# Moving the mLSTM value transposes between other tiles of TensorE, and splitting the last head's x in two spans

## The chip, the cores and the metric

The kernel runs on one core of a Trainium2 chip. The metric is the device time of one execution in microseconds. Before the change the median of three runs is 2675.86 us (2675.53 to 2677.09).

## The reference, cut to what matters

The model is two blocks in a row on 512 tokens of width 1024. The first is an RWKV-7 layer and a forgetting-attention layer with their MLPs. The second is an mLSTM layer followed by a Fourier layer. The change touches only the first stage of the mLSTM layer, which computes, for each of 4 heads of width 512 and for 768 tokens (256 context and 512 latent ones):

```
xm     = h @ w_in                       # per head: 512 channels x 768 tokens
xconv  = silu(conv3x3(xm) + b)          # depthwise; context tokens as one row
q, k   = xconv @ w_q, xconv @ w_k       # scores = (q k^T), latent queries x all keys
v      = xm                             # values, needed with tokens on the partitions
gates  = q @ wq_g + k @ wk_g + v @ wv_g # input and forget gates
```

The chunked scan with gates, the output norm and the projection follow in a later stage. The kernel keeps channels on the partitions, folds w_q and w_k into one 512 x 512 matrix per head (so that scores are xconv^T (W xconv)), and must transpose xm to get the values.

## The kernel before, in words

All large products are computed in three passes of a split precision: each operand is a high part (fp32r) and a low part (what the high part leaves), and hi*hi, hi*lo and lo*hi are summed in PSUM. So each activation needs two instructions, one that writes the high part (ScalarE) and one that subtracts it (VectorE or GpSimd), and GpSimd does the same for the weights: `whi` (L500), then `wlo` (L502), a ring of two blocks.

**The stage.** It is one block of the program, from about 1641 us to 1933 us of the profiled execution. Each engine has its own list, written out in program order, and the engines meet at semaphores only. For head h = 0..3, TensorE does:

1. "xm" of head h+1: 8 tiles (4 groups m of 128 channels, each with a 256-token and a 512-token tile), 24 matmuls per tile (L554), from two weight blocks. Head 0's own tiles were made before the loop.
2. "v" of head h: 6 tiles of 4 fp32 transposes each (L2774), a tile being 128 tokens x 512 channels.
3. "q" of head h: 4 tiles of 12 matmuls (L2784), from `xch` and `xcl`, the high and low parts of the convolved x.
4. The gate sums of head h, 24 groups in PSUM banks 4 and 5 (L2798).
5. "s", the scores of head h: 6 tiles (one per 128 keys) of 12 matmuls (L2806), from `xch`, `xcl` as weights and `qk_h`, `qk_l`.

All tiles but the gate sums go through a ring of four PSUM banks (NACC = 4), in the order of the list `order`. A tile may begin when the tile four places ahead of it in that list has been taken: `acc_taken` counts reads by ScalarE, and `low_made` counts the low parts of q by VectorE.

**ScalarE** reads xm tiles out (L2815, `xm_tile`), then the value tiles: it needs a row sum first, so that vsb = 512 * v - sum(v). For head 0 it makes the sum itself (L2875, with an accumulated output) and then the read (L2878). For heads 1 and 2 VectorE makes the sum (`value_sum`, L2981). For head 3, VectorE does both for tiles 0 and 1, and the sums of the others. Then ScalarE sends `vsb` to DRAM, makes the high parts of q (L2833), reads the scores (L2815 again) and between the last four of them does `silu` of the next head (L2823) with its DMA; after all six it makes `xch` of the next head (`high_x`, L2828, four instructions over all 768 tokens).

**VectorE** makes the low parts `xcl` (L2992, heads 1 and 2), then the convolution of the next head, four groups m of eleven instructions on PSUM banks 6 and 7 (L2958, L2957) and a copy (L2972). Inside the group m = 2 of the heads 1 and 2 the six `value_sum` stand between the taps, and inside m = 3 the four `low_of` of q (L3002). After them come the gate sums (L3031). For head 3, where no convolution is left, it waits for the last score of head 2 (`taken("s", h - 1, 5)`), then does value tiles 0 and 1, `xcl` of groups 2 and 3, and the other sums. GpSimd makes `xcl` of head 0, and of head 3's groups 0 and 1 (L2719).

So head 3's x, of which TensorE reads the same `xch`/`xcl` buffers as head 2, can be split only when the last score of head 2 is done, and q of head 3 waits for that.

Of the kernel before, what the change touches and what calls it, by code (L numbers as in the profile page):

```python
# [377 lines left out]
def program(nc, A, out, plan, vat, cat):  # L378
    ctx = ExitStack()
    with ctx:  # L380
# [2281 lines left out]
        read_place = {what: j for j, what in enumerate(w for w in order if w not in low_place)}  # L2662
        phase_start()
        with nc.Block() as block:
# [17 lines left out]
            head_gates_in = signal("head_gates_in")  # L2682

# [32 lines left out]
            def _(pool):  # L2716
# [12 lines left out]
                low(3, 0)  # L2729
                low(3, 1)  # L2730
# [3 lines left out]
            def _(pe):  # L2734
# [13 lines left out]

                def xm_of(h):
                    for j in range(2):  # L2750
                        if h == 0 and j == 0:
                            block_by_tile(pe, firsts["xm0"][1], h2h, h2l, h_ready, tokens=spans, bank_free=bank_free)
                            continue
                        block_of(pe, firsts[f"xm{h}"][1] + j, 0, h2h, h2l, KT, 256, tokens=spans, bank_free=bank_free)
# [12 lines left out]
                for h in range(HM):  # L2767
# [1003 lines left out]
```

## Time and profile before

| | us |
|---|---|
| median of 3 runs | 2675.86 |
| the profiled execution's own time | 2674.32 |
| its span (first to last instruction) | 2672.5 |
| TensorE (PE) busy | 2551.9 (95%) |
| VectorE (DVE) busy | 1309.9 (49%) |
| ScalarE (ACT) busy | 734.8 (27%) |
| GpSimd (POOL) busy | 1462.3 (55%) |
| mean granted TensorE clock | 0.973 of full |

Rows of the timeline give the start, the duration, the engine and line, what is written from what, and in brackets how long the engine had been idle and which instruction released it. Matmuls overlap their successors, so the time that one costs is the distance between two starts (0.227 us for 512 columns in this stage) and not its duration (0.39 us).

### The profile page before, as it was taken

The numbers are of one execution on the slowest core, as the hardware profiler recorded it, in microseconds if no ns is written. First come the engines' busy times: TensorE is split into PE (matmuls) and PEld (weight loads), VectorE is DVE, ScalarE is ACT, GpSimd is POOL, SyncE is SP. The second block draws the span as 40 slices with busy tenths as digits, with TensorE's granted clock in tenths as the row PEclk, the third lists the DMA queues.
The fourth block names the chain that finished last, engine by engine and source line by source line (L and its number), as shares of the span: only waits on it lengthen the run. The fifth ranks groups of instructions, "written<-read, shape, count | busy, mean of one in ns | idle before, by whom it ended". The sixth has DMA issues, their size and how long they took to land. (4 is left out here: it accounts for less than half of the span.)

```text
span 2672.5 us, 36710 instructions
## 1 busy us (share of the span) xinstructions
PE 2551.9 (95%) x15042; PEld 2037.0 (76%) x15042; DVE 1309.9 (49%) x1880; ACT 734.8 (27%) x1381; POOL 1462.3 (55%) x472
## 2 busy tenths in 40 slices
PE   5899989999999999999999999999899999999998
PEld 4677778788888886657888887788676578877787
DVE  7737337675662241453845526977285634131212
ACT  4644332231120221452311212323323422011210
POOL 3663633477777665206777763433272037754674
PEclk9999989999999999999999998999999999999999
DMA  6221433656653221103555522222243345222121
GB/s 270 96 73 60 121 92 155 271 216 230 230 220 110 87 103 65 69 1 130 210 214 218 214 99 97 103 111 111 103 166 113 129 166 229 95 79 77 64 101 72
DMA packets 89903, 358.80 MB, mean 134 GB/s; under 512 B 27288, under 2 KB 41112, under 8 KB 52384
## 3 DMA queue, kind: packets, MB, share of 16 engines
q1 hardware_dynamic: 64992, 227.65, 23.8%
q10 hardware_dynamic: 24768, 129.12, 12.9%
q8 instruction: 106, 1.74, 0.3%
q14 instruction: 37, 0.30, 0.0%
HBM read 317.66 MB, written 39.06 MB: 133 GB/s over the span
## 5 line engine op out<-in xcount | busy, mean ns | idle before, releaser
L500 POOL TENSOR_TENSOR whi<-wraw,con_sb 128x2048 fp32r<-128x2048 f32 x166 | 600.2, 3616 | 1072.2 <-PE ps L554 755.9
L502 POOL TENSOR_TENSOR wlo<-wraw,whi 128x2048 fp32r<-128x2048 f32 x166 | 783.0, 4717 | 13.0
L554 PE MATMUL ps<-hh,whi 128*128 128x512 f32 x952 | 373.0, 392 | 6.0 <-POOL wlo L502 6.0
L554 PE MATMUL ps<-hh,wlo 128*128 128x512 f32 x952 | 371.4, 390 | 0.0
L554 PE MATMUL ps<-hl,whi 128*128 128x512 f32 x952 | 371.4, 390 | 0.0
L554 PEld LDWEIGHTS ps<-hh,whi 128*128 128x128 f32 x952 | 179.4, 188 | 47.4 <-POOL wlo L502 6.4
L2165 DVE TENSOR_TENSOR midl<-rsq,midh 128x512 fp32r<-128x512 f32 x64 | 155.9, 2441 | 112.6 <-ACT midh L2122 112.6
L554 PEld LDWEIGHTS ps<-hh,wlo 128*128 128x128 f32 x952 | 179.3, 188 | 37.5
L554 PEld LDWEIGHTS ps<-hl,whi 128*128 128x128 f32 x952 | 179.5, 189 | 37.0
L554 PE MATMUL ps<-midh,whi 128*128 128x512 f32 x512 | 200.0, 391 | 0.0
L554 PE MATMUL ps<-midh,wlo 128*128 128x512 f32 x512 | 199.7, 390 | 0.0
L554 PE MATMUL ps<-midl,whi 128*128 128x512 f32 x512 | 199.6, 390 | 0.0
L554 PE MATMUL ps<-h2h,whi 128*128 128x512 f32 (+1 forms) x480 | 177.9, 371 | 0.7 <-ACT hb L3307 0.7
L554 PE MATMUL ps<-h2l,whi 128*128 128x512 f32 (+1 forms) x480 | 176.6, 368 | 0.0
L554 PE MATMUL ps<-h2h,wlo 128*128 128x512 f32 (+1 forms) x480 | 176.5, 368 | 0.0
L2025 DVE SCALAR_TENSOR_TENSOR cond_w<-cond_w,ps 128x1024 f32<-128x1024 f32 x136 | 159.8, 1210 | 0.0
L2116 ACT ACTIVATE relu<-ps 128x512 f32<-128x512 f32 x64 | 38.2, 598 | 381.2 <-PE ps L554 347.9
L2171 DVE SCALAR_TENSOR_TENSOR x<-ps,mod,x 128x512 f32<-128x512 f32 x64 | 48.0, 750 | 190.5 <-PE ps L554 190.5
L554 PEld LDWEIGHTS ps<-midl,whi 128*128 128x128 f32 x512 | 96.5, 189 | 20.1
L554 PEld LDWEIGHTS ps<-midh,wlo 128*128 128x128 f32 x512 | 96.4, 188 | 20.1
L554 PEld LDWEIGHTS ps<-midh,whi 128*128 128x128 f32 x512 | 96.5, 189 | 19.9
L2957 DVE SCALAR_TENSOR_TENSOR ps<-xm,vec_sb,ps 128x441 f32<-128x441 f32 (+3 forms) x160 | 105.0, 656 | 4.8
(477 smaller groups left out, 4804.8 us busy)
## 6 DMA issues: line engine op xcount, KB each, us to landing
wraw<-wst SPq DMA_DIRECT2D x162, 1024.0 KB, 4.8
cond_w<-wcond ACTq DMA_DIRECT2D x68, 1024.0 KB, 4.8
first_w<-wcond SPq DMA_DIRECT2D x8, 1024.0 KB, 19.6
mod_w<-wcond SPq DMA_DIRECT2D x8, 1024.0 KB, 13.9
d_v<-key_and_query ACTq DMA_DIRECT2D x4, 1536.0 KB, 5.7
d_s<-ssb ACTq DMA_DIRECT2D x4, 1536.0 KB, 5.3
sld<-d_s SPq DMA_DIRECT2D x4, 1536.0 KB, 8.3
vld<-d_v SPq DMA_DIRECT2D x16, 384.0 KB, 3.5
```

Of the source, the lines that this page charges most:

```text
L500: pool.tensor_tensor(whi[:, s], wraw[:, f], C("zero").broadcast_to([P, BLK]), ALU.add).then_inc(sem("w_high"), 1)
L502: pool.tensor_tensor(wlo[:, s], wraw[:, f], whi[:, s].bitcast(F32), ALU.subtract).then_inc(w_split, 1)
L554: o = e.matmul(ps[:, b, :nt], w[:, k, mc], x[:, k0 + k, t0:t0 + nt], start=first and k == 0 and j == 0, stop=final and k == nk - 1 and j == 2)
L2025: o = dve.scalar_tensor_tensor(cond_w[n % 2][:, m], cond_w[n % 2][:, m], 1.0, row_at[r], ALU.mult, ALU.mult, accum_out=cond_to[layer][2 * ...
L2116: act.activation(relu[:, n % 4], ps[:, b], ACT.Relu).then_inc(*AC.up(acc_free[b]))
L2165: dve.tensor_tensor(midl[n // KT % 2][:, n % KT], rsq[:, n % 4], midh[n // KT % 2][:, n % KT].bitcast(F32), ALU.subtract).then_inc(*mid_lo ...
L2171: dve.scalar_tensor_tensor(x_sb[:, m], ps[:, b], mod[layer][:, 40 + m:41 + m], x_sb[:, m], ALU.mult, ALU.add).then_inc(*VE.up(acc_free[b]))
L2957: dve.scalar_tensor_tensor(dst, src, w(kh, kw), dst, ALU.mult, ALU.add).then_inc(*VE.up(chain))
```

## The change

- The values of heads 0, 1 and 2 are transposed two tiles at a time behind the groups m = 1, 2, 3 of the next head's xm tiles. ScalarE makes sum and read of them all, in the same order; VectorE's `value_sum` leaves the convolution.
- The values of head 3 are transposed one tile at a time behind each of head 2's score tiles. VectorE sums and reads them (`last_value_taken`).
- The scores of head 2 are done in the order 2, 3, 4, 5 (latent keys), 0, 1 (context keys). The `silu` of head 3 stand behind the first four. The high part of its x is made in two spans: the 512 latent tokens after the fourth score has been read, the 256 context tokens after the sixth. VectorE makes the low parts in the same two spans (`last_lows`), with value tiles 4 and 5 between them. GpSimd makes none of head 3.
- q of head 3 waits for the latent low parts, k by k; the gate sums wait for the context low parts. xm blocks are issued in four quarters instead of two halves.

```diff
         order = [("xm", 0, n) for n in range(8)]
+        V_BEHIND = {1: (0, 1), 2: (2, 3), 3: (4, 5)}
+        def score_order(h):
+            return (2, 3, 4, 5, 0, 1) if h == HM - 2 else range(6)
         for h in range(HM):
-            order += [("xm", h + 1, n) for n in range(8) if h + 1 < HM]
-            order += [(what, h, n) for what, many in (("v", 6), ("q", 4), ("s", 6)) for n in range(many)]
+            for m in range(4):
+                if h + 1 < HM:
+                    order += [("xm", h + 1, 2 * m), ("xm", h + 1, 2 * m + 1)]
+                    order += [("v", h, n) for n in V_BEHIND.get(m, ())]
+            order += [("q", h, n) for n in range(4)]
+            for i, n in enumerate(score_order(h)):
+                order += [("s", h, n)] + [("v", HM - 1, i)] * (h == HM - 2)
...
+                if (what, h) == ("v", HM - 1):
+                    return last_value_taken.at(n + 1)
...
-                low(3, 0)
-                low(3, 1)
                 split_weights(pool, ahead(*names)[1])
...
+                    for m in range(4):
+                        block_of(pe, firsts[f"xm{h}"][1] + m // 2, 0, h2h, h2l, KT, 256, tokens=spans, m0=m % 2, mn=1,
+                                 tell=m % 2 == 0, bank_free=bank_free)
+                        for n in V_BEHIND.get(m, ()):
+                            turn_values(h - 1, n)
...
-                    for s in range(6):
-                        b = tile_bank()
-                        for m in range(4):
-                            o = pe.transpose(ps[:, b, P * m:P * m + P], xm[:, m, P * s:P * s + P], ident)
-                        o.then_inc(*PE.up(acc_ready))
-                    pe.wait_ge(*PE.need(sem("xc_ready"), 4))
+                    if h < HM - 1:
+                        pe.wait_ge(*PE.need(sem("xc_ready"), 4))
...
+                            if h == HM - 1 and m == 0:
+                                pe.wait_ge(*last_low[0].at(k + 1))
...
+                    if h == HM - 1:
+                        pe.wait_ge(*last_low[1].at(4))
...
-                    for s in range(6):
+                    for i, s in enumerate(score_order(h)):
...
+                        if h == HM - 2:
+                            turn_values(HM - 1, i)
...
+                def value_read(h, n):
+                    b = bank()
+                    act.wait_ge(*AC.need(acc_ready))
+                    act.activation(vsb[:, n], ps[:, b], ACT.Copy, scale=-1.0,
+                                   accum_out=vsum[:, n:n + 1]).then_inc(*v_summed.inc())
+                    act.wait_ge(*v_summed.at(6 * h + n + 1))
+                    act.activation(vsb[:, n], ps[:, b], ACT.Identity, bias=vsum[:, n:n + 1],
+                                   scale=512.0).then_inc(*AC.up(acc_taken))
...
+                        if h == HM - 2:
+                            AC.skip(acc_ready, 1)
+                            turn["evac"] += 1
+                            if i < 4:
+                                silu(h + 1, i)
+                            if i == 3:
+                                for m in range(4):
+                                    high_x(m, LAT)
...
-                        if h:
-                            conv(h + 1, 2, lambda s: value_sum(h, s))
-                        else:
-                            conv(1, 2)
+                        conv(h + 1, 2)
                         conv(h + 1, 3, lambda n: low_of("q", h, n))
                     else:
-                        dve.wait_ge(*taken("s", h - 1, 5))
-                        for s in range(2):
-                            value_sum(h, s)
-                            value_read(h, s)
-                        low(h, 2)
-                        low(h, 3)
-                        for s in range(2, 6):
-                            value_sum(h, s)
+                        for n in range(4):
+                            value_sum(h, n)
+                            value_read(h, n)
+                        last_lows(0, LAT)
+                        for n in range(4, 6):
+                            value_sum(h, n)
+                            value_read(h, n)
+                        last_lows(1, CX)
```

TensorE in the scores of head 2, before: the end of the last score tile (`qk_h`, `qk_l`, `xch`, `xcl`), the values of head 3 (24 transposes of `xm_12908`) and the first matmuls of its q (L2784).

```order
L2806 MATMUL ps<-qk_h,xch 128x512
L2806 MATMUL ps<-qk_l,xch 128x512
L2806 MATMUL ps<-qk_h,xcl 128x512
L2774 MATMUL ps<-con_sb,xm_12908 128x128 x24
L2784 MATMUL ps<-xch,whi 128x512
L2784 MATMUL ps<-xcl,whi 128x512
L2784 MATMUL ps<-xch,wlo 128x512
```

After the change, the same engine in the scores of head 2 (L2830 is the score line now, L2766 the transpose line):

```order
L2830 MATMUL ps<-qk_h,xch 128x512
L2830 MATMUL ps<-qk_l,xch 128x512
L2830 MATMUL ps<-qk_h,xcl 128x512
L2766 MATMUL ps<-con_sb,xm_12908 128x128 x4
L2830 MATMUL ps<-qk_h,xch 128x512
L2830 MATMUL ps<-qk_l,xch 128x512
L2830 MATMUL ps<-qk_h,xcl 128x512
L2830 MATMUL ps<-qk_h,xch 128x512
L2830 MATMUL ps<-qk_l,xch 128x512
L2830 MATMUL ps<-qk_h,xcl 128x512
```

The 24 transposes of head 3 stand in six groups of four behind the six score tiles, and q begins behind the last group. In the same way each of the three groups of 24 transposes of heads 0 to 2 is now three groups of eight between xm tiles.

VectorE at the end of the stage, before: the two sums and reads of value tiles 0 and 1 (`key_and_query` is the buffer of the values), two low parts of x, four sums, and the first low part of q:

```order
L2981 TENSOR_REDUCE vsum<-ps 128x1
L2987 TENSOR_SCALAR key_and_query<-ps,vsum 128x512
L2981 TENSOR_REDUCE vsum<-ps 128x1
L2987 TENSOR_SCALAR key_and_query<-ps,vsum 128x512
L2992 TENSOR_TENSOR xcl<-xc_third,xch 128x768
L2992 TENSOR_TENSOR xcl<-xc_fourth,xch 128x768
L2981 TENSOR_REDUCE vsum<-ps 128x1 x4
L3002 TENSOR_TENSOR qk_l<-ps,qk_h 128x512 x4
```

And after the change, from the sum of value tile 3 on:

```order
L3016 TENSOR_REDUCE vsum<-ps 128x1
L3022 TENSOR_SCALAR key_and_query<-ps,vsum 128x512
L3029 TENSOR_TENSOR xcl<-xc,xch 128x512 x2
L3029 TENSOR_TENSOR xcl<-xc_third,xch 128x512
L3029 TENSOR_TENSOR xcl<-xc_fourth,xch 128x512
L3016 TENSOR_REDUCE vsum<-ps 128x1
L3022 TENSOR_SCALAR key_and_query<-ps,vsum 128x512
L3016 TENSOR_REDUCE vsum<-ps 128x1
L3022 TENSOR_SCALAR key_and_query<-ps,vsum 128x512
L3029 TENSOR_TENSOR xcl<-xc,xch 128x256 x2
L3029 TENSOR_TENSOR xcl<-xc_third,xch 128x256
L3029 TENSOR_TENSOR xcl<-xc_fourth,xch 128x256
```

All six sums and reads are VectorE's now, and the eight low parts are those of 512 latent tokens, then those of 256 context tokens, with value tiles 4 and 5 between them.

## Rows read from the trace of the kernel before

**Rows 1.** Part 1 of the page: busy time of each engine, share of the span.

```profile
PE 2551.9 (95%) x15042; PEld 2037.0 (76%) x15042; DVE 1309.9 (49%) x1880; ACT 734.8 (27%) x1381; POOL 1462.3 (55%) x472
```

**Rows 2.** Waits of TensorE, 1700 to 1933 us: total, times, longest.

```profile
PE ps L2784 <- ACT key_and_query L2878: 7.3, 4, 5.7
...
PE ps L2806 <- DVE qk_l L3002: 0.3, 1, 0.3
```

**Rows 3.** Timeline of TensorE: first value transposes and first q matmul, heads 0, 1, 3.

```profile
1710.68 1.91 PE L2774 MATMUL ps<-con_sb,xm 128*128 128x128 f32 x16
...
1715.52 0.47 PE L2784 MATMUL ps<-xch,whi 128*128 128x512 f32 x1 [0.73 <-ACT key_and_query L2878]
...
1780.84 1.91 PE L2774 MATMUL ps<-con_sb,xm 128*128 128x128 f32 x16
...
1785.46 0.47 PE L2784 MATMUL ps<-xch,whi 128*128 128x512 f32 x1 [0.32 <-ACT key_and_query L2878]
...
1886.61 1.91 PE L2774 MATMUL ps<-con_sb,xm 128*128 128x128 f32 x16
...
1896.69 0.77 PE L2784 MATMUL ps<-xch,whi 128*128 128x512 f32 x1 [5.67 <-ACT key_and_query L2878]
```

**Rows 4.** Timeline of ScalarE: the value sums of two tiles of head 0.

```profile
1711.38 0.59 ACT L2875 ACTIVATE key_and_query<-ps 128x512 f32<-128x512 f32 x1
...
1712.68 0.59 ACT L2875 ACTIVATE key_and_query<-ps 128x512 f32<-128x512 f32 x1
```

**Rows 5.** Timeline of TensorE: gate sums and first scores, heads 0, 1, 2, 3.

```profile
1726.61 0.64 PE L2798 MATMUL ps<-xm,value_gate 128*32 128x256 f32 x8
...
1731.01 0.50 PE L2806 MATMUL ps<-qk_h,xch 128*128 128x512 f32 x1 [0.32 <-DVE qk_l L3002]
...
1800.55 0.50 PE L2806 MATMUL ps<-qk_h,xch 128*128 128x512 f32 x1
...
1869.57 0.61 PE L2798 MATMUL ps<-xcl,folded_w 128*32 128x512 f32 x4
1870.11 0.50 PE L2806 MATMUL ps<-qk_h,xch 128*128 128x512 f32 x1
1870.45 0.40 PE L2806 MATMUL ps<-qk_l,xch 128*128 128x512 f32 x1
...
1910.65 0.64 PE L2798 MATMUL ps<-xm,value_gate 128*32 128x256 f32 x8
```

**Rows 6.** Timeline of VectorE: the last low part of q, heads 0 and 1.

```profile
1730.27 0.68 DVE L3002 TENSOR_TENSOR qk_l<-ps,qk_h 128x512 fp32r<-128x512 f32 x1
...
1797.28 0.69 DVE L3002 TENSOR_TENSOR qk_l<-ps,qk_h 128x512 fp32r<-128x512 f32 x1 [0.21 <-ACT qk_h L2833]
```

**Rows 7.** Windows, busy time by engine, clock: head 0 of the convolution, head 1's transposes.

```profile
1661.00:1735.00 74.00, 72.06 (x423) 59.95 (x423) 70.14 (x101) 24.84 (x45) 40.12 (x12) 1.00 0.32 118
...
1781.00:1786.00 5.00, 3.60 (x27) 2.83 (x25) 4.52 (x8) 2.78 (x5) 0.00 (x0) 1.00 0.01 2
```

**Rows 8.** Timeline of VectorE, 1750 us: three low parts of x in head 1.

```profile
1750.86 6.78 DVE L2992 TENSOR_TENSOR xcl<-xc,xch 128x768 fp32r<-128x768 f32 x2 [15.18 <-ACT xch L2828]
1757.56 0.95 DVE L2992 TENSOR_TENSOR xcl<-xc_third,xch 128x768 fp32r<-128x768 f32 x1
```

**Rows 9.** Timeline of GpSimd, same time: high and low part of a weight block.

```profile
1747.92 3.60 POOL L500 TENSOR_TENSOR whi<-wraw,con_sb 128x2048 fp32r<-128x2048 f32 x1 [23.45 <-PE ps L554]
1751.60 5.22 POOL L502 TENSOR_TENSOR wlo<-wraw,whi 128x2048 fp32r<-128x2048 f32 x1
```

**Rows 10.** Timeline of TensorE: two other idle times, at 2040 and 1992 us.

```profile
1992.18 0.80 PE L3211 MATMUL ps<-con_sb,gnat 4*128 4x4 f32 x6 [3.31 <-DVE nm L3474]
...
2040.69 1.10 PE L3193 MATMUL ps<-pp,vld 128*128 128x512 f32 x2 [2.39 <-DVE pp L3438]
```

**Rows 11.** Windows, granted clock right behind those idle times (third number from the end).

```profile
1992.00:1996.00 4.00, 3.82 (x24) 2.63 (x24) 0.36 (x2) 0.00 (x0) 0.00 (x0) 0.50 0.24 92
...
2040.70:2042.00 1.30, 1.08 (x2) 0.25 (x2) 1.23 (x3) 0.00 (x0) 0.00 (x0) 1.00 0.34 114
```

More of the change, by code:

```diff
@@ L2661, in program @@
         low_place = {what: j for j, what in enumerate(parted_tiles)}
-        read_place = {what: j for j, what in enumerate(w for w in order if w not in low_place)}
+        read_place = {what: j for j, what in enumerate(
+            w for w in order if w not in low_place and w[:2] != ("v", HM - 1))}
         phase_start()
@@ L2682, in program @@
             head_gates_in = signal("head_gates_in")
+            last_value_taken = signal("last_value_taken")
+            last_low = [signal(f"last_low_made{j}") for j in range(2)]
             h_items = [("ctx", k) for k in range(KT)] + [("lat", k) for k in range(KT)]
@@ L2747, in tile_bank, with turn_values @@
                     return b
-                def xm_of(h):
[L2750 to L2754, printed above, removed]
+                def turn_values(h, n):
+                    b = tile_bank()
+                    for m in range(4):
+                        o = pe.transpose(ps[:, b, P * m:P * m + P], xms[h % 2][:, m, P * n:P * n + P], ident)
+                    o.then_inc(*PE.up(acc_ready))
+                def xm_of(h):
+                    if h == 0:
+                        block_by_tile(pe, firsts["xm0"][1], h2h, h2l, h_ready, tokens=spans, bank_free=bank_free)
+                        block_of(pe, firsts["xm0"][1] + 1, 0, h2h, h2l, KT, 256, tokens=spans, bank_free=bank_free)
+                        return
+                    for m in range(4):
[3 more added lines that the diff above has]
+                            turn_values(h - 1, n)
                 fold_product(pe, 14, 0)
@@ L2864, in _ @@
                             high_x(m + 2)
-                    if h:
-                        act.wait_ge(*AC.need(sem("v_sent"), 16))
-                    for s in range(6):
-                        b = bank()
-                        act.wait_ge(*AC.need(acc_ready))
-                        if h == HM - 1 and s < 2:
-                            continue
-                        if h == HM - 1 and s == 2:
-                            act.wait_ge(*taken("v", h, 1))
-                        if h == 0:
-                            act.activation(vsb[:, s], ps[:, b], ACT.Copy, scale=-1.0,
-                                           accum_out=vsum[:, s:s + 1]).then_inc(*v_summed.inc())
-                        act.wait_ge(*v_summed.at(6 * h + s + 1))
-                        act.activation(vsb[:, s], ps[:, b], ACT.Identity, bias=vsum[:, s:s + 1],
-                                       scale=512.0).then_inc(*AC.up(acc_taken))
+                        if h + 1 < HM and m in V_BEHIND:
+                            if h and m == 1:
+                                act.wait_ge(*AC.need(sem("v_sent"), 16))
+                            for n in V_BEHIND[m]:
+                                value_read(h, n)
                     act.wait_ge(*taken("v", h, 5))
@@ L2885, in _ @@
                         act.wait_ge(*AC.need(sem("s_sent"), 16))
-                    for s in range(6):
+                    for i, s in enumerate(score_order(h)):
                         read_out(ssb[:, s], T, scale=KS)
-                        if h + 1 < HM and s >= 2:
+                        if h == HM - 2:
[4 more added lines that the diff above has]
+                            if i == 3:
+                                for m in range(4):
+                                    high_x(m, LAT)
+                        elif h + 1 < HM and s >= 2:
                             silu(h + 1, s - 2)
-                    act.wait_ge(*taken("s", h, 5))
+                    if h == HM - 2:
+                        for m in range(4):
+                            high_x(m, CX)
+                    act.wait_ge(*taken("s", h, score_order(h)[5]))
                     act.dma_start(d_s[h], ssb[:]).then_inc(*AC.up16(sem("s_sent")))
-                    if h + 1 < HM:
+                    if h + 2 < HM:
                         for m in range(4):
@@ L2974, in value_sum @@
                 def value_sum(h, s):
-                    if s >= 6:
-                        return
                     n = place["v", h, s]
@@ L2987, in value_read, with last_lows @@
                     dve.tensor_scalar(vsb[:, s], ps[:, place["v", h, s] % NACC], 512.0, vsum[:, s:s + 1], ALU.mult,
-                                      ALU.add).then_inc(*VE.up(acc_taken))
+                                      ALU.add).then_inc(*last_value_taken.inc())
+                def last_lows(j, part):
+                    for m in range(4):
+                        dve.wait_ge(*xc_high(HM - 1 + j, m))
+                        dve.tensor_tensor(xcl[:, m, part], xcs[m][:, part], xch[:, m, part].bitcast(F32),
+                                          ALU.subtract).then_inc(*last_low[j].inc())
                 def low(h, m):
```

6 lines of the change are left out of this document (3 added, 3 removed).

## The prediction

> **What bounds the kernel now.** I read the page's busy times first: TensorE (PE) is busy 2551.9 us, 95% of the span, and no other engine reaches 56% [rows 1]. So a change is worth what it takes from TensorE's idle time and from its time at the low clock, unless another engine then decides. Second I read TensorE's own waits inside the stage that the change touches: of all its idle time, the largest item is at the first matmul of q (L2784), 7.3 us in four waits, the longest 5.7, all for ScalarE's reads of the value tiles. At the scores only 0.3 us is waited, for VectorE's low part of q [rows 2]. Third, the timeline around these places gives what each costs.
>
> From the first transpose of a head to the first matmul of its q it takes 1715.52 - 1710.68 = 4.84 us in head 0, 4.62 us in head 1, and 1896.69 - 1886.61 = 10.08 us in head 3 [rows 3]. Head 2 repeats head 1 to the hundredth, so there are two of 4.62. The transposes themselves need little of it: sixteen take 1.91 us when nothing holds them [rows 3], so 24 take at most 2.87; since 1.91 contains the last one's tail once, I estimate 2.62 us. The rest is the ring of four banks: a value tile is made in some 0.44 us (a sixth of 2.62), but read by ScalarE only every 1.30 us, from 1711.38 to 1712.68 [rows 4].
>
> **The change part by part.**
>
> *Heads 1 and 2, values behind the xm tiles.* The same 24 transposes are issued per head, so 2.62 us stay. What goes is the wait: 4.62 - 2.62 = 2.0 us a head. What is late next? ScalarE now makes sum and read of two tiles, 2 x 1.30 = 2.6 us, in each of three groups of TensorE work that last 24 x 0.12 + 24 x 0.227 = 8.3 us plus eight transposes of 0.9; with the two xm reads of about 1 us it is less than half busy. The ring asks that a tile four places back was read: behind value tiles it is the xm pair of the same group, and for the next pair it is the xm pair of the group before. Before q the four tiles are xm 6, xm 7, v 4 and v 5, and q's third tile, the first that needs v 4, begins 5.4 us after q starts. So no bank holds TensorE, and I cost the ring at nothing; if that cover were gone the price is 1.3 us a tile.
>
> The other thing that can be late is VectorE. In head 1 its last low part of q ended at 1797.28 + 0.69 = 1797.97, and the scores began at 1800.55 [rows 5, 6]: 2.6 us of slack. TensorE comes 1.6 us earlier by my sum, and VectorE loses six sums over 512 columns in the convolution before it; a low part of q has as many columns and takes 0.69 us [rows 6], so they are some 3.6 us with their overlap. The slack stays positive.
>
> *Switching.* New are the places where fp32 transposes hand over to fp32r matmuls. The nearest case: four gate matmuls begin at 1869.57, the first score matmul at 1870.11, the second at 1870.45 [rows 5]. A score's tail is 0.40 - 0.227 = 0.17 us, so of the four gate matmuls' 0.61 us some 0.44 is work, and without a handover the second score would be at 1869.57 + 0.44 + 0.227 = 1870.24: it costs about 0.21 us. The other end is nothing (for the way in, from matmuls to transposes, I take nothing). I take 0.2 us. Heads 1 and 2 get two more handovers each, 0.4 us: 2.0 becomes 1.6 us a head, 3.2 us for both.
>
> *Head 0.* Here the gain is lost, I think. VectorE is busy 70.14 of 74 us from 1661 to 1735 with 101 instructions, the rest being the 0.04 us between them [rows 7]: it runs the convolutions of heads 0 and 1 back to back, and q's low parts stand between the taps of the last one. The fourth begins at 1730.27 whatever TensorE does, and the scores at 1731.01 wait for it [rows 5, 6]. TensorE's gate sums ended 0.32 us before, at 1730.69; after the change they end 4.84 - 2.62 - 0.4 = 1.8 us earlier, at 1728.9, and it idles 2.1 us (2.5 without handover costs). Nothing gained, and an idle time that may cost the clock (below).
>
> *Head 3.* The 10.08 us become six transposed tiles between the scores of head 2: 2.62 us of work and five more handovers, 1.0 us. 10.08 - 3.62 = 6.46 us. Then the clock. q of head 3 took 1910.65 - 1896.69 = 13.96 us against 1726.61 - 1715.52 = 11.09 in head 0 [rows 3, 5], because after the 5.67 us of idle it began at the lower of the two clock levels, 1.2 GHz. That is 2.87 us which go with the idle time. Sum 9.3 us.
>
> For this q must not wait. Its four latent low parts are ready in time: behind the fourth score ScalarE has a read, a silu over 768 columns with its DMA and four high parts of 512 tokens. By the 0.59 us of an instruction over 512 columns [rows 4] I estimate six times that and 0.6 for silu's width and the DMA, 4.2 us, with VectorE's last low part near 4.9; TensorE has two scores and three value tiles left, 6.8 us. A value tile of head 3 takes VectorE two instructions over 512 columns, some 1.4 us, against 3.2 us for a score with its value tile on TensorE.
>
> The context low parts are closer. VectorE makes them from 1.5 us after q began, just when GpSimd splits the next weight block. In head 1 two low parts of 768 tokens took 6.78 us beside such a split, L500 for 3.60 and L502 for 5.22; the next one, alone, took 0.95 [rows 8, 9]. So one slips in between L500 and L502 and three come after, at about 0.4 each for 256 tokens: done about 10.4 us after q began. The gate sums want them at 10.9. The Trainium skill (SBUF — State Buffer, section "SBUF: two separate sides") says that the port pair which VectorE and GpSimd share is locked for a whole instruction and the loser blocks fully; the trace agrees, and if the bandwidth were shared instead the parts would be done by about 4 us. By either, the sum is the same. The nearest row for an upper end is 0.95 us apiece behind both GpSimd instructions, 9.7 + 3.8 = 13.5: then 2.4 us are lost.
>
> *Sum.* 3.2 + 0 + 9.3 = 12.5 us. The profiled execution took 2674.32 us (span 2672.5 and 1.8 around it); it becomes 2661.8. It lies 1.5 us under the median of the runs, 2675.86, so the forecast for the median is 2663.4.
>
> With no handover cost it is 14.3 (2661.5). Everything behind the stage shifts with it: its first VectorE chain starts with the stage's last gate sum, and the DMAs that it reads were sent earlier.
>
> **The rivals.**
>
> *A. The idle time in head 0 costs the clock.* 2.1 to 2.5 us of idle before head 0's scores lies between what rows show. An idle time of 3.31 us was followed by 1.2 GHz at once, one of 2.39 us resumed at full clock [rows 10, 11]. If it falls, the dense work behind it loses at most the 2.87 us of head 3, whose idle time was more than twice as long, and I put half of it, 1.4, as the lower end; I take 2.0. Time: 2665.4. For it: the idle is nearly as long as the longer one, and the gate sums before it use columns by quarters. Against: the 2.39 us row is the nearest.
>
> *B. The context low parts come late*, by the 2.4 us worked out above, and q's low parts behind them by less than their slack. 2665.8.
>
> *C. VectorE decides in heads 1 and 2 as it does in head 0.* Then their 3.2 us are lost: 2666.6. For it: the convolution there also follows x's low parts, which are slow beside GpSimd. Against: the 2.6 us of slack and the six sums that leave.
>
> *D. Slower: the transposes cost the clock.* Before, 24 of them stand in one place per head; now fifteen groups interrupt dense work. If a group of transposes made the clock fall, the matmuls behind each would lose 2.0 us as in A: 15 x 2.0 = 30 us more, 2693, slower than before. It decides when a fall follows groups of 0.4 to 0.9 us. Against: the whole stretch of head 1's transposes, with its idle time, 1781 to 1786 us, shows the clock at 1.00 with PE busy 3.60 of 5 us [rows 7]. The Trainium skill (TensorE: Matmul & The Clock Gate, "Part 4: PE-mode transpose") says that the full clock does not engage for transposes, since they do not count as busy in the same way. By that rule the groups would be short holes in dense work; here no row shows a fall behind so short a hole, so it gives D its small chance.
>
> *E. The change does not do what it says*: TensorE still stops at q, for instance for the weight block of q or for a bank. The price of one such stop a head is about 2 us: 2669.
>
> **How the numbers follow.** Forecast 0.52 (2663.4, own range 2661.5 to 2664.8), A 0.30, B 0.06, C 0.05, E 0.05, D 0.02. What a measurement of this kernel can tell from no change is 0.2%, 5.4 us: below 2670.5 is faster. All cases but D and the bad half of E lie below. Faster 0.95, same 0.03, slower 0.02. The range takes in the forecast without handover costs and some luck with clock levels elsewhere (2660.3) and reaches over A, B and C with their upper prices (2667.5).
>
> **What would show it.** In the profile after: the first q matmul of heads 1 and 2 follows the last transpose or matmul without a wait; head 0's scores wait 2 to 2.5 us for VectorE's low part of q; head 3's q takes 11.1 us at clock 1.00 and starts with no wait; a handover costs 0.1 to 0.25 us; the stage from its first matmul to the last score is 12.5 us shorter. Wrong would be: a wait at L554 for a value read (the ring), a wait at the gate sums of head 3 of over 0.5 us (B), a clock of 0.50 behind head 0's wait (A) or inside the xm tiles (D).

## The result and the profile after

The changed kernel takes 2658.97 us (median of 4 runs, 2657.66 to 2663.04). The kernel before took 2675.87 beside it (2675.53 to 2677.09). The ratio is 0.994, with a 95% interval from 0.9928 to 0.9952: it is faster by 16.9 us. The forecast was 2663.4 with a range from 2660.3 to 2667.5, so the time lies 1.3 us below the range.

Part 1 of the page after, which answers to [rows 1]:

```profile
PE 2545.2 (96%) x15042; PEld 2032.7 (76%) x15042; DVE 1313.5 (49%) x1878; ACT 739.5 (28%) x1405; POOL 1457.8 (55%) x470
```

TensorE has as many matmuls as before and is busy for 6.7 us less: part of the gain is not idle time but the granted clock, at which the same matmuls are shorter. The span fell from 2672.5 to 2657.5 us.

I cut both traces at two places: the first matmul of the changed stage (head 0's xm), and the gate-sum transposes that follow the last score. The first two rows are windows of the kernel before, the stage and what lies behind it. The columns are length; busy time and count of PE, PEld, DVE, ACT and POOL; granted clock; DMA share; GB/s.

```profile
1641.16:1932.76 291.60, 278.55 (x1536) 227.97 (x1537) 196.61 (x268) 88.76 (x145) 103.20 (x28) 0.97 0.28 105
1932.80:2672.50 739.70, 714.70 (x3182) 548.34 (x3182) 269.64 (x444) 166.98 (x325) 391.85 (x94) 0.98 0.33 119
```

The same two windows of the changed kernel:

```profile
1642.52:1921.41 278.89, 274.78 (x1537) 226.69 (x1537) 200.60 (x266) 93.48 (x169) 98.98 (x26) 0.98 0.29 110
1921.40:2657.50 736.10, 710.90 (x3182) 545.38 (x3182) 269.57 (x444) 166.93 (x325) 391.69 (x94) 0.98 0.33 119
```

The stage went from 291.60 to 278.89 us, 12.7 less (12.5 were forecast). What lies behind it, which the change does not touch and where the counts are the same, went from 739.7 to 736.1 us with 3.8 us less of busy TensorE. Ahead of the stage the changed kernel was 1.4 us later, in code that is the same.

Waits of TensorE between 1695 and 1922 us in the changed kernel, which answer to [rows 2] (engine, line and releaser; total, times, longest):

```profile
PE ps L2830 <- DVE qk_l L3044: 2.7, 1, 2.7
PE ps L3243 <- PEq L2676: 1.5, 1, 1.5
```

The 7.3 us at q are gone, and so are 4.0 us inside the groups of transposes (2.8 for ScalarE's reads and 1.2 for VectorE's, in the same view of before). One wait of 2.7 us has come: head 0's scores for VectorE's last low part of q. The 1.5 us stand at the end of the stage, as before. The timeline of TensorE shows the new wait, and the scores behind it:

```profile
1728.67 1.04 PE L2822 MATMUL ps<-xcl,folded_w 128*32 128x512 f32 x8
1732.36 0.50 PE L2830 MATMUL ps<-qk_h,xch 128*128 128x512 f32 x1 [2.65 <-DVE qk_l L3044]
...
1733.16 0.39 PE L2830 MATMUL ps<-qk_h,xch 128*128 128x512 f32 x1
...
1734.54 0.63 PE L2830 MATMUL ps<-qk_l,xch 128*128 128x512 f32 x1
```

About a microsecond after TensorE started again, its matmuls take 0.63 us instead of 0.39. The window of these scores tells why (third number from the end):

```profile
1733.50:1737.00 3.50, 3.50 (x10) 2.71 (x9) 3.40 (x6) 0.09 (x1) 0.00 (x0) 0.51 0.00 0
```

This is 1.2 GHz, the lower of the two levels. The kernel before stood at 1.00 in its scores of head 0.

The handovers in heads 1 and 2, and in the scores of head 2 (timeline of TensorE after):

```profile
1776.35 1.03 PE L2766 MATMUL ps<-con_sb,xm 128*128 128x128 f32 x8
1777.14 0.36 PE L554 MATMUL ps<-h2h,whi 128*128 128x256 f32 x1
1777.34 0.28 PE L554 MATMUL ps<-h2l,whi 128*128 128x256 f32 x1
1777.46 0.28 PE L554 MATMUL ps<-h2h,wlo 128*128 128x256 f32 x1
...
1785.57 1.03 PE L2766 MATMUL ps<-con_sb,xm 128*128 128x128 f32 x8
1786.36 0.48 PE L2806 MATMUL ps<-xch,whi 128*128 128x512 f32 x1
...
1881.45 0.60 PE L2766 MATMUL ps<-con_sb,xm 128*128 128x128 f32 x4
1881.80 0.48 PE L2830 MATMUL ps<-qk_h,xch 128*128 128x512 f32 x1
1882.12 0.40 PE L2830 MATMUL ps<-qk_l,xch 128*128 128x512 f32 x1
```

Read the starts: eight transposes take 0.79 us from their first to the next fp32r matmul, four take 0.35. The first matmul behind them holds the next for 0.08 us more than usual (0.20 instead of 0.12, or 0.32 instead of 0.23). So a group pays 0.09 to 0.1 us per transpose and 0.08 for the handover, not 0.2.

Head 3. The low parts (VectorE, then GpSimd) and the start of q and of the gate sums (TensorE):

```profile
1888.49 0.69 DVE L3016 TENSOR_REDUCE vsum<-ps 128x1 f32<-128x512 f32 x1 [0.47 <-PE ps L2766]
1889.22 0.75 DVE L3022 TENSOR_SCALAR key_and_query<-ps,vsum 128x512 f32<-128x512 f32 x1
1889.88 2.77 DVE L3029 TENSOR_TENSOR xcl<-xc,xch 128x256 fp32r<-128x256 f32 x1
...
1897.67 0.41 DVE L3029 TENSOR_TENSOR xcl<-xc_fourth,xch 128x256 fp32r<-128x256 f32 x1
```

```profile
1888.77 3.60 POOL L500 TENSOR_TENSOR whi<-wraw,con_sb 128x2048 fp32r<-128x2048 f32 x1 [26.06 <-PE ps L2806]
1892.45 4.68 POOL L502 TENSOR_TENSOR wlo<-wraw,whi 128x2048 fp32r<-128x2048 f32 x1
```

```profile
1888.21 0.48 PE L2806 MATMUL ps<-xch,whi 128*128 128x512 f32 x1
...
1899.29 0.64 PE L2822 MATMUL ps<-xm,value_gate 128*32 128x256 f32 x8
```

A part of 0.41 us took 2.77 beside the first GpSimd instruction, the next one lasted until 1897.4 beside the second, and the last ended at 1898.08: 9.9 us behind the start of q (forecast 10.4), 1.2 us before the gate sums. TensorE waits for neither; q took 11.08 us, at full clock.

Behind the stage, the idle time ahead of the scan's small matmuls, which answers to [rows 10], and the clock behind it, to [rows 11] (timeline and windows of TensorE after):

```profile
1980.79 0.53 PE L3250 MATMUL ps<-con_sb,gnat 4*128 4x4 f32 x6 [3.33 <-DVE nm L3513]
```

```profile
1980.79:1982.30 1.51, 1.51 (x22) 1.51 (x24) 0.02 (x1) 0.00 (x0) 0.00 (x0) 1.00 0.52 199
1983.00:1989.00 6.00, 6.00 (x15) 4.45 (x14) 1.90 (x2) 4.40 (x7) 4.57 (x2) 0.50 0.00 0
```

Before, 3.31 us of idle were followed by 1.2 GHz at once, and six matmuls took 0.80 us. Now 3.33 us are followed by 2.4 GHz for 1.5 us, the same six take 0.53, and the clock falls only then, for about 7 us instead of 10. Nothing in the instructions has changed here, and the fall itself has not gone: it comes later and is shorter. Two other places behind the stage differ too. First the kernel before: 32 narrow matmuls of one column each, the window of a short fall that follows them at 2179 us, and that of a long fall at 2347 us:

```profile
2174.44 3.67 PE L3175 MATMUL ps<-con_sb,hsq 128*128 128x1 f32 x32
...
2179.50:2182.50 3.00, 3.00 (x8) 2.31 (x7) 0.00 (x0) 1.30 (x3) 2.92 (x2) 0.50 0.00 0
...
2347.00:2356.00 9.00, 6.21 (x18) 5.08 (x19) 6.62 (x11) 3.48 (x6) 7.99 (x2) 0.50 0.31 104
```

The fall at 2179 follows no idle time: the last one ended at 2163.42, 16 us before. After, it does not happen (its place is near 2167 us now), and the long one lasts about 7 us instead of 10:

```profile
2160.00:2175.00 15.00, 15.00 (x87) 13.18 (x87) 2.90 (x5) 4.49 (x7) 8.20 (x2) 1.00 0.20 72
...
2334.00:2342.00 8.00, 5.55 (x16) 4.34 (x16) 7.77 (x12) 4.09 (x6) 6.60 (x2) 0.57 0.32 116
```

By the starts of the same matmuls in both traces, the three places give 1.53, 1.67 and 0.92 us, and the rest 0.5 the other way: 3.65 us.

### The profile page after: what moved, and what is told of

It is laid out like the page before. It is cut to its first block and busy times, and to the rows that moved or that the text cites. A ratio compares the mean times of both kernels' runs of the same rounds, so it can differ in the third digit from the quotient of the medians.

```text
span 2657.5 us, 36713 instructions
## 1 busy us (share of the span) xinstructions
PE 2545.2 (96%) x15042; PEld 2032.7 (76%) x15042; DVE 1313.5 (49%) x1878; ACT 739.5 (28%) x1405; POOL 1457.8 (55%) x470
## 3 DMA queue, kind: packets, MB, share of 16 engines
q10 hardware_dynamic: 24768, 129.12, 12.9%
```

## The experiments

Each ratio is to the kernel before on the same chip. The medians of that kernel alone differ by 1.3 us between chips (2674.53 to 2675.87), and the executions of one edited program by 1.3 to 6 us, with their granted clocks (the changed kernel in the first comparison: spans 2655.8 to 2661.2 us, clocks 0.975 and 0.976). So the verdicts rest on the two lengths read from each profile, the stage and the part behind it. Each profile is one execution, so each length is one sample.

### The changed kernel again

Nothing is edited. Open was whether the shorter part behind was luck of one execution.

> The changed kernel once more, unchanged, for more runs and a second profile. Theory 1 (the stage gives 12.7 us, the rest of the first comparison is where the clock levels happened to fall): the stage, from its first xm matmul to the gate sum transposes behind the last score, lasts 278.9 us if the clock falls behind head 0's wait and 277.3 us if it doesn't; the time behind the stage, with the same waits, is not 736.1 us again but differs from it by 0.5 to 4 us, and goes with the time at the low clock. Theory 2 (something behind the stage became shorter for good, 3.65 us): behind the stage 736.1 us again, within 0.3.

Measured: 2659.89 us (2659.8 to 2661.19, 5 runs), ratio 0.9945 [0.9932, 0.9959]. Stage 279.01, part behind 736.05, where theory 1 wanted another length. Two profiles out of two make luck of one execution unlikely. The two are not the same inside: in the second the clock fell for 3.5 us in the scan instead of 7, and not at all near 2031 us, where the first has 3.5 us of low clock. The 1.6 us won in the scan are gone by 2011 us, where matmuls that VectorE feeds start no earlier than in the first profile. So equal lengths do not mean equal clocks.

### Heads 0 to 2 alone

Values of heads 0 to 2 placed between the xm tiles; head 3 as before. The edit against the changed kernel, cut:

```diff
-            order += [("q", h, n) for n in range(4)]
-            for i, n in enumerate(score_order(h)):
-                order += [("s", h, n)] + [("v", HM - 1, i)] * (h == HM - 2)
+            if h == HM - 1:
+                order += [("v", h, n) for n in range(6)]
+            order += [(what, h, n) for what, many in (("q", 4), ("s", 6)) for n in range(many)]
...
```

> Only the values of heads 0 to 2 are moved between xm tiles; the last head is as before. Theory 1: heads 1 and 2 shorter by 2.08 us each, head 0 by nothing with 1.6 us lost if the clock falls behind its 2.6 us wait; head 3 keeps its 10.1 us and its low clock. Stage 291.6 - 4.2 + 1.6 = 289.0 us (287.4 without the fall), time about 2673. Rival (the gain of the change needs the value reads of heads 0 to 2 out of the way before the last head): the last head changes too, 2668 or less.

Measured: 2672.41 us (2670.23 to 2674.91, 11 runs), ratio 0.999 [0.9981, 0.9999]. Stage 288.66, part behind 739.95. So this part gives 2.9 us of the stage: twice 2.07 in heads 1 and 2, nothing in head 0, and 1.6 lost to the clock in head 0's scores. (The rest is 0.4 us less in head 3's q.)

### The last head alone

Head 3 as in the change; heads 0 to 2 as before, with their 24 transposes together ahead of q.

```diff
-                        for n in V_BEHIND.get(m, ()):
-                            turn_values(h - 1, n)
+                    for n in range(6):
+                        turn_values(h - 1, n)
...
```

> Only the last head's part: its values between head 2's scores, scores reordered, x in two spans; the values of heads 0 to 2 as before. Theory 1: scores of head 2 with the values 19.3 us instead of 26.6, q and gate sums of head 3 15.1 instead of 18.0: 10.2 us, no fall in head 0 since VectorE's low part is waited for 0.3 us only. Stage 281.4 us, time about 2665.6. Rival (the parts need one another): q of head 3 waits again, time 2669 or more.

Measured: 2665.4 us (2662.99 to 2667.97, 5 runs), ratio 0.9964 [0.9951, 0.9978]. Stage 281.65, part behind 740.13. So head 3 alone makes the stage 9.95 us shorter. The two parts alone make 12.9 us of stage, the change 12.7: they add up. But each alone leaves the part behind at 740 us, and together they shorten it. That speaks against a cause in the code of either part alone.

### All six values of heads 0 to 2 behind the last xm group

```diff
-        V_BEHIND = {1: (0, 1), 2: (2, 3), 3: (4, 5)}
+        V_BEHIND = {3: (0, 1, 2, 3, 4, 5)}
...
-                            if h and m == 1:
+                            if h and m == 3:
```

> The changed kernel with all six value tiles of heads 0 to 2 behind the last group of xm tiles, ScalarE making sum and read of all. If the gain in heads 1 and 2 is that of the ring (a value tile read every 1.30 us), they get 2.3 us longer each, 4.84 us from first transpose to q as head 0 had; head 0 waits 0.3 us for VectorE instead of 2.65 and keeps its clock, 1.6 us back. Sum 3.0 us over the changed kernel: stage 281.9 us, time about 2662. Rival (the gain came from VectorE's six sums that left the convolution): heads 1 and 2 stay as in the changed kernel, stage 277.3, time 2657.5.

Measured: 2666.38 us (2664.28 to 2668.03, 7 runs), ratio 0.9969 [0.9958, 0.998]. Stage 281.86, as expected; part behind 740.28, which is most of why the time is 4 us over the expectation. The timeline of TensorE in head 1 has all the waits back (brackets: idle time and releaser):

```profile
1782.09 0.66 PE L2766 MATMUL ps<-con_sb,xm 128*128 128x128 f32 x4 [0.25 <-ACT key_and_query L2863]
1783.39 0.66 PE L2766 MATMUL ps<-con_sb,xm 128*128 128x128 f32 x4 [0.64 <-ACT key_and_query L2863]
1784.78 0.47 PE L2806 MATMUL ps<-xch,whi 128*128 128x512 f32 x1 [0.73 <-ACT key_and_query L2863]
```

Value tiles follow each other every 1.30 us, the pace of ScalarE. VectorE's sums are out of the convolution here too, so it is the spacing that takes the wait away.

### The last head's high parts after all six scores

The four high parts of the latent tokens are made behind the sixth score of head 2 instead of the fourth.

```diff
-                            if i == 3:
+                            if i == 5:
                                 for m in range(4):
                                     high_x(m, LAT)
```

> The changed kernel, but the latent high parts of head 3's x are made after the sixth score of head 2 instead of after the fourth. q of head 3 then waits for them. Theory 1 (simple): four high parts at 0.5 us behind the last read, the first low part 1.4 us after q could start: q waits about 1.5 to 2 us. Theory 2 (the low parts collide with GpSimd's split of a weight block, which the first q matmul sets off, as they do in head 1): low parts 2 to 4 are blocked during L500 (3.6 us) and L502 (4.6 us), so q and the gate sums lose 5 to 9 us. Time by theory 1 about 2661.5, by theory 2 2664 to 2669.

Measured: 2668.21 us (2664.94 to 2670.97, 11 runs), ratio 0.9975 [0.9966, 0.9984]. Stage 284.57, 5.7 us more than the change; part behind 737.54. The profiled execution is the fastest of the eleven, 3.3 us under their median. First the timeline of VectorE, then that of TensorE in q of head 3:

```profile
1887.71 1.29 DVE L3029 TENSOR_TENSOR xcl<-xc,xch 128x512 fp32r<-128x512 f32 x2 [5.64 <-ACT xch L2854]
1888.93 0.68 DVE L3029 TENSOR_TENSOR xcl<-xc_third,xch 128x512 fp32r<-128x512 f32 x1
1889.53 4.08 DVE L3029 TENSOR_TENSOR xcl<-xc_fourth,xch 128x512 fp32r<-128x512 f32 x1
```

```profile
1888.56 0.47 PE L2806 MATMUL ps<-xch,whi 128*128 128x512 f32 x1 [1.59 <-DVE xcl L3029]
1893.67 0.50 PE L2806 MATMUL ps<-xch,whi 128*128 128x512 f32 x1 [2.81 <-DVE xcl L3029]
1895.06 0.50 PE L2806 MATMUL ps<-xch,whi 128*128 128x512 f32 x1 [0.42 <-DVE key_and_query L3022]
```

The fourth low part meets GpSimd's split, which began at 1889.10 us, and takes 4.08 us instead of 0.68. TensorE stands for 4.8 us in three places. The split in two spans with the early latent one is thus worth 5.7 us, over half of head 3's gain, and what it avoids is in the larger part that meeting.

### Head 0's low parts of q earlier

VectorE makes the four low parts of head 0's q one group of taps earlier.

```diff
-                        conv(h + 1, 2)
-                        conv(h + 1, 3, lambda n: low_of("q", h, n))
+                        if h:
+                            conv(h + 1, 2)
+                            conv(h + 1, 3, lambda n: low_of("q", h, n))
+                        else:
+                            conv(1, 2, lambda tap: low_of("q", 0, (tap - 3) // 2) if tap in (3, 5, 7) else None)
+                            low_of("q", 0, 3)
+                            conv(1, 3)
```

> The changed kernel with the four low parts of head 0's q placed in and right behind the convolution group before the last (m = 2) instead of in the last (m = 3). The 2.65 us wait before head 0's scores goes, and with it the clock fall behind it (1.6 us): stage 278.9 - 4.2 = 274.7 us. Theory 1 (the 3.65 us behind the stage came for good): time about 2655. Theory 3 (the part behind the stage is 736.1 us or about 740 us long according to where the stage's end falls against the clock's changes; the changed kernel, 12.7 us shorter, falls well, the three kernels that were 2.9, 9.7 and 10.0 us shorter fall badly): 16.9 us shorter falls badly again, behind the stage 739.5 to 740.5 us, time 2658 to 2660, no gain.

Measured: 2659.4 us (2657.91 to 2660.41, 5 runs), ratio 0.9942 [0.9929, 0.9956]. Stage 274.56: the wait of 2.7 us and the low clock behind it are gone, 4.3 us. Part behind 740.06: 4.0 us more than the change. Its timeline at the start of head 0's scores has no wait, and that of the scan's small matmuls has 0.80 again:

```profile
1727.61 1.04 PE L2822 MATMUL ps<-xcl,folded_w 128*32 128x512 f32 x8
1728.58 0.50 PE L2830 MATMUL ps<-qk_h,xch 128*128 128x512 f32 x1
...
1975.42 0.80 PE L3255 MATMUL ps<-con_sb,gnat 4*128 4x4 f32 x6 [3.28 <-DVE nm L3518]
```

So a true gain of 4.3 us shows as none in the time.

### Eight useless transposes at the end of the stage

In the kernel before, and in the version with head 0's early low parts:

```diff
+                for _pad in range(8):
+                    pe.transpose(ps[:, 7, :P], xms[(HM - 1) % 2][:, 0, :P], ident)
```

> The kernel before with eight more transposes (about 0.85 us of work with no use, into a free bank of PSUM) behind the last score of head 3. Theory 1 (work on TensorE's path is paid for): 0.85 us slower, 2676.4, behind the stage 739.7 us. Theory 3: stage 292.5 us, the end of the stage falls as in the changed kernel, behind it 736 us: faster than before by 2.8 us, 2672.7.

> Head 0's low parts early and the same eight useless transposes behind the last score. Theory 1: 0.85 us slower than without them. Theory 3: stage 275.5 us, behind it 736 us instead of 740: about 3 us faster than without them, 2655.5, and the fastest kernel so far.

Measured: 2674.65 us (2673.1 to 2678.1, 11 runs), ratio 0.9999 [0.999, 1.0008], stage 291.63, behind 739.70; and 2657.75 us (2653.55 to 2659.38, 5 runs), ratio 0.9931 [0.9918, 0.9945], stage 274.58, behind 740.04. Neither length moved, so these two do not test theory 3; they show that eight more instructions alone switch nothing. The timeline of the second shows why:

```profile
1914.44 1.03 PE L2836 MATMUL ps<-con_sb,xm 128*128 128x128 f32 x8
1916.06 1.53 PE L3250 MATMUL ps<-gacc,con_sb 128*128 128x256 f32 x4 [0.58 <-PEq L2676]
```

TensorE's own queue holds the first instruction of the next block for 1.45 us; with the transposes 0.58 are left of it, and the stage's end stays. They also serve as repeats: in all three pairs of profiles that differ by nothing on the path the part behind is the same to 0.04 us.

### Useless transposes on the path

Put ahead of the last head's second score tile, where TensorE waits for nothing: nine or five in the version with head 0's early low parts, nine in the kernel before, 26 in the changed kernel.

```diff
                     for i, s in enumerate(score_order(h)):
                         b = tile_bank()
+                        for _pad in range(9 if h == HM - 1 and i == 1 else 0):
+                            pe.transpose(ps[:, b, :P], xms[h % 2][:, 0, :P], ident)
```

> The version that makes the low parts of head 0's q earlier (stage 274.56 us, part behind it 740.06, span 2656.1), with nine useless transposes ahead of the second score tile of the last head, where TensorE waits for nothing: 9 x 0.099 = 0.9 us on the path (eight transposes and the handover took 0.79). Theory 3 (where the end of the stage falls against the changes of the clock decides whether the part behind takes 740 or 736.1): its end moves to where the changed kernel's end falls against them, so stage 275.45, part behind 736.1, span 2653.0, that is about 3 us FASTER than without the useless work. Rival (the part behind is short for a reason of the change's own code, which this version has lost with its earlier low parts, or the 736.1 of two profiles belongs to that program alone): part behind 740.1, span 2657.0, slower by 0.9.

> The kernel before (stage 291.60 us, part behind it 739.74, span 2672.5) with the same nine useless transposes ahead of the last head's second score tile. Theory 3: stage 292.5, part behind 736.1, span 2669.7, faster than before by 2.8 us although it only has more to do. Rival (the short part behind belongs to the change's code): part behind 739.8, span 2673.4, slower by 0.9.

> The changed kernel (stage 278.89 us, part behind it 736.09, span 2657.5) with 26 useless transposes ahead of the last head's second score tile: 26 x 0.099 = 2.57 us. Theory 3: its end comes to stand against the clock's changes where the kernel before has it, so stage 281.5, part behind 740.0, span 2664.0, slower than the changed kernel by 6.5 us for 2.6 us of work. Rival (the short part behind belongs to the change's code): part behind 736.1, span 2660.1, slower by 2.6.

> As the run with nine useless transposes in the version with head 0's early low parts, but with five: 5 x 0.099 = 0.5 us, which brings the stage's end to where the variant with all values behind the last group had it against the clock's changes (its part behind was 740.28). Theory 3: part behind still 740.1, span 2656.6, so that the four transposes between this kernel and the one with nine are worth 3.6 us the other way. Rival: part behind the same as in the one with nine whatever it is there, span 0.4 us below that one.

Measured, with the kernels that they start from (us; the last column is the duration of the six small matmuls behind the idle time of 3.3 us):

| | time (ratio) | stage | behind | six |
|---|---|---|---|---|
| before | | 291.60 | 739.74 | 0.80 |
| before, nine | 2672.92 (0.9992 [0.9983, 1.0001]) | 292.59 | 735.84 | 0.53 |
| the change | 2658.97 (0.994 [0.9928, 0.9952]) | 278.89 | 736.09 | 0.53 |
| the change, 26 | 2666.17 (0.9963 [0.9949, 0.9977]) | 281.75 | 740.03 | 0.80 |
| early low parts | 2659.40 (0.9942 [0.9929, 0.9956]) | 274.56 | 740.06 | 0.80 |
| the same, five | 2660.13 (0.9945 [0.9931, 0.9959]) | 275.16 | 740.34 | 0.80 |
| the same, nine | 2657.62 (0.9931 [0.9917, 0.9944]) | 275.60 | 736.23 | 0.53 |

All four parts behind are where theory 3 put them, within 0.3 us, and the rival is out in all four. The kernel before is given 1.0 us of useless work and its stage and the part behind it become 2.9 us shorter together. The changed kernel is given 2.9 us and loses 6.8. Nine transposes in place of five make the stage 0.4 us longer and the part behind it 4.1 us shorter. The medians go the same way: all five executions with 26 are slower than all nine of the changed kernel, and all five with nine faster than all five with five. For the kernel before the gain is 1.6 us, and the interval of its ratio just reaches 1. The spans came out 1.4 to 2.8 us over the expectations, mostly since these profiles reached the stage later (1642.50 to 1643.97 us instead of 1641.16 to 1642.52), in code that is the same.

Two windows side by side, each 1.5 us from the first matmul behind the idle time. The version with nine:

```profile
1978.93:1980.43 1.50, 1.50 (x22) 1.50 (x24) 0.00 (x1) 0.00 (x0) 0.00 (x0) 1.00 0.57 220
```

The changed kernel with 26:

```profile
1984.73:1986.23 1.50, 1.50 (x14) 1.50 (x15) 0.00 (x0) 0.00 (x0) 0.00 (x0) 0.50 0.53 206
```

The same instructions, behind the same idle time of 3.3 us, at 2.4 and at 1.2 GHz. What differs is when the idle time comes. The start in the span alone does not order the results: the part behind began at 1921.95 us and took 736.05, and at 1922.12 in another program and took 740.28. The length of the stage does, in alternating groups: 274.56 to 275.16 us go with 740, 275.60 and 278.9 to 279.0 with 736, 281.65 to 281.86 with 740, 284.57 with 737.5, 288.66 to 291.63 with 740, 292.59 with 736.

## Why the prediction was wrong

The forecast for the profiled execution was 2661.8 us, and it took 2659.37: 2.4 less. The stage gave 0.2 more than forecast, the part behind it 3.65 more, and the part ahead 1.4 less. The median of the runs then came 0.4 us below the profiled execution, where I had added 1.5 as for the kernel before; that is the other 1.9 us.

**The step that failed** is "Everything behind the stage shifts with it". The waits there did shift as they were, the work is the same, but the granted clock did not shift with them. The part behind takes 740 us in nine profiles (before among them), 736 in four (the change twice, and two with useless work), and 737.5 in one, that with the late high parts: it has the early fall at the scan's small matmuls, as the 740s, and lacks the two later losses. The runs with 0.4 to 2.9 us of useless work switched it to and fro. With 739.74 in place of 736.09 the median would have been 2662.6, inside the range. The second term is the 1.5 us added from the profiled execution to the median: it came as 0.4 the other way, with four executions that spread over 5.4 us. Had it held, 2660.9 would lie just inside too; it took both to leave the range. The trace of before had the first term: low clock behind idle times of 3.3, 2.4 and 0.8 us, and behind the narrow matmuls at 2174 us, in a stretch that was about to be moved by 12 us. My range gave this only "some luck", down to 2660.3. What the runs do not give is a rule for when the switch happens, and none is offered here.

**Heads 1 and 2**: the mechanism was right, the size was not. The gain is 2.07 us a head, not 1.6. The term "I take 0.2 us" for a handover was too high, with "2.62 us" for the transposes: three groups take 3 x 0.79 = 2.37 us and 0.16 for two slower starts behind them.

**Head 0**: right. Nothing is gained (TensorE reaches the scores 2.3 us earlier and waits), and the idle time is 2.65 us, a little over the 2.1 to 2.5.

**Rival A** happened, and was given 0.30. Its price was 2.0 us; the scores of head 0 took 18.08 instead of 16.46 us, 1.6. I had held against it that 2.39 us of idle was followed by full clock [rows 10, 11]. That was read too short: the window ends 1.3 us behind the idle time, and the clock of the kernel before fell just behind it, from about 2042.8 us:

```profile
2043.00:2046.30 3.30, 3.30 (x5) 1.19 (x5) 3.09 (x11) 0.00 (x0) 0.00 (x0) 0.52 0.00 0
```

In the run with the late high parts, 2.81 us of idle at 1893.67 had no fall behind it, here or up to 1920 us:

```profile
1893.70:1899.00 5.30, 4.88 (x20) 3.74 (x21) 5.23 (x8) 1.20 (x2) 4.37 (x1) 1.00 0.35 148
```

A fall of about 3.5 us stands behind the 2.39 us in 13 of the 14 profiles, 1.5 to 2.5 us late and with another 0.86 us of idle between. All five profiles with head 0's wait (2.65 to 2.68 us) have the fall about a microsecond late, and the 3.3 us has one in all 14, at once or 1.5 to 2 us late. So A deserved more than 0.30, though the 2.81 us shows that length alone does not settle it.

**Head 3**: right in the wait and in the clock, 7.29 us for the place of the values (forecast 6.46; the handovers and transposes were again priced too high) and 2.88 for the clock in q (forecast 2.87). Its low parts came as forecast, so B did not happen.

**The sum** of 12.5 against 12.7 hides two errors that cancel: heads 1 to 3 gave 1.8 us more, and A took 1.6.

**C, D and E** did not happen. For D, the window of head 1's xm tiles with all three groups of transposes in it, and that of the last score and values of head 2:

```profile
1762.00:1797.00 35.00, 35.00 (x191) 30.20 (x190) 32.31 (x47) 12.20 (x27) 16.46 (x4) 1.00 0.26 100
...
1881.30:1889.00 7.70, 7.70 (x42) 6.36 (x41) 5.80 (x9) 5.04 (x10) 0.23 (x1) 1.00 0.11 40
```

Both stand at 2.4 GHz. The Trainium skill (TensorE: Matmul & The Clock Gate, "Part 4: PE-mode transpose") holds that transposes do not engage the full clock. As short groups between dense matmuls they did not cost it in this kernel, and even the 26 in a row took 2.75 us at a granted clock of 1.00.

**Which version is fastest?** From the stage's first matmul to the end, the changed kernel takes 1015.0 us, the one with early low parts 1014.6, and that with nine useless transposes 1011.8. In medians these three are 2658.97, 2659.40 and 2657.62, with overlapping ratios: the profiles tell them apart, the times do not.

## What to carry to other kernels

When a change shortens one stage, also cut the trace behind it and compare the unchanged part, with its granted clock: here 3.65 of 16.9 us came from there, and a real gain of 4.3 us disappeared there. A range for a change that shifts a stretch with idle times should take in the clock falls near them at full price, in both directions. To tell a gain of the code from such a shift, put a microsecond or less of useless work on the path and look whether the result jumps. And read the clock for several microseconds behind an idle time: here the falls behind idle times of 2.4 and 2.7 us came 1 to 2.5 us after them, where my window had ended.

## What the runs showed of the hardware

- A stretch of the same instructions and the same waits took about 736 or 740 us, the same in both profiles where a program was profiled again (736.09 and 736.05) or with nothing added on the path (740.06 and 740.04), according to how long the stage ahead of it was (275.16 us: 740.34; 275.60 us: 736.23). An idle time of 3.3 us was followed by 1.2 GHz at once or after at least 1.5 us of 2.4 GHz.
- The clock fell behind idle times of 3.3 us (14 of 14 profiles), 2.65 to 2.68 (5 of 5) and 2.39 with another 0.86 (13 of 14), at once or up to 2.5 us late; it did not behind 2.81 us in the one profile that has it. In nine profiles it also fell 0.5 to 1.5 us behind 32 matmuls of one column each, with no idle time.
- Going from fp32 transposes to fp32r matmuls costs about 0.08 us, at the second matmul. A transpose of 128 x 128 takes about 0.1 us in a row.
- TensorE's queue took 1.45 us to pass from one block of the program to the next, and 0.8 us of transposes at the end of the block did not delay it.
- One low part of 128 x 512, 0.68 us alone, took 4.08 us beside GpSimd's split of a weight block.
